# Block attention in four PSUM banks, stepped beside three gate projections; stage boundaries handed over by token half

## The reference

```python
# first block: an MLA mixer and an mLSTM mixer, each followed by
x = _layernorm(ALPHA * x + y, ln_w[layer], ln_b[layer])
...
# second block
mod = c_act @ w_ada[l] + b_ada[l]
sh1, sc1, g1, sh2, sc2, g2 = [m[:, None, :] for m in jnp.split(mod, 6, axis=-1)]
h = rms_norm(x, norm1_w[l]) * (1.0 + sc1) + sh1
proj = h @ w_in[l]
qa, ka, va, qb, kb, vb, ga, gb = jnp.split(proj, offs, axis=-1)
...
ya = global_gqa(qa, ka, va)
yb = neighbourhood_attention(qb, kb, vb, nat_rpb[l])     # reshapes left out
merged = jax.nn.sigmoid(ga) * (ya @ w_oa[l]) + jax.nn.sigmoid(gb) * (yb @ w_ob[l])
x = x + g1 * (merged @ w_out[l])
h2 = rms_norm(x, norm2_w[l]) * (1.0 + sc2) + sh2
ff = (jax.nn.silu(h2 @ w_ffn_gate[l]) * (h2 @ w_ffn_up[l])) @ w_ffn_down[l]
x = x + g2 * ff
```

## Time and profile before

| | |
|---|---|
| median of 3 runs | 2306.06 us (2302.61 to 2310.73) |
| the profiled execution | 2306.09 us |
| its span, first to last instruction | 2304.4 us |
| mean granted clock of PE | 0.981 of full speed |
| busy: PE, PEld, DVE, ACT, POOL | 2233.5, 1884.6, 1495.8, 1007.7, 243.3 us |
| HBM read | 495.34 MB, 216 GB/s |

### The profile page before, as it was taken

How to read it: one execution, slowest core, us unless ns; L and a number is a source line. 1 busy time by engine, 2 the same in 40 slices (tenths; PEclk the granted TensorE clock), 3 DMA queues, 4 the chain that set the end, 5 groups by cost and what they waited for, 6 DMA issues and landing times.

```text
span 2304.4 us, 33253 instructions
## 1 busy us (share of the span) xinstructions
PE 2233.5 (97%) x11044; PEld 1884.6 (82%) x11044; DVE 1495.8 (65%) x1990; ACT 1007.7 (44%) x1248; POOL 243.3 (11%) x425
## 2 busy tenths in 40 slices
PE   8999998999999979999999999999999999999996
PEld 7888776998877769799778888888888888888885
DVE  5666578887776866777676667775665565454544
ACT  5444534454444433434554443444444444343432
POOL 1110011212220030100111111110110010000000
PEclk9999999999999997999999999989999999999998
DMA  8786166887986583767538887755677676665663
GB/s 307 248 242 175 37 228 256 249 265 264 318 278 180 159 243 122 247 184 226 193 106 273 254 261 245 235 207 179 223 256 228 220 258 217 190 206 183 190 197 119
DMA packets 196666, 499.25 MB, mean 217 GB/s; under 512 B 29784, under 2 KB 56536, under 8 KB 195648
## 3 DMA queue, kind: packets, MB, share of 16 engines
q1 hardware_dynamic: 163648, 388.03, 52.3%
q0 software_dynamic: 32896, 109.55, 14.3%
HBM read 495.34 MB, written 2.10 MB: 216 GB/s over the span
## 4 chain that ended last, share of the span: by engine, by line
PE 89%; DVE 4%; DMA 3%; ACT 2%; issue 1%; POOL 0%; DVEq 0%; POOLq 0%; SPq 0%; ACTq 0%
PE ps L1669 72%; PE ps L1678 10%; PE ps L1738 2%; PE ps L1759 1%; DMA ada_raw<-in_w_ada_dram 1%; PE ps L1748 1%; DMA raw<-in_ml_w_in_dram 1%; DVE lo L924 1%; DMA rel<-in_rpbT_dram 1%; PE ps L1829 1%; PE ps L1912 0%; PE ps L1707 0%; DVE acc_g L936 0%; ACT hi L551 0%; PE ps L1968 0%
## 5 line engine op out<-in xcount | busy, mean ns | idle before, releaser
L924 DVE TENSOR_TENSOR lo<-raw,hi 128x1024 fp32r<-128x1024 f32 x732 | 892.8, 1224 | 616.9 <-ACT hi L551 614.6
L551 ACT CAST hi<-raw 128x1024 fp32r<-128x1024 f32 x732 | 765.9, 1051 | 1080.4 <-PE ps L1669 848.2
L1669 PE MATMUL ps<-hi,XH 128*128 128x512 f32 x2080 | 650.6, 393 | 28.8 <-DVE lo L924 22.3
L1669 PE MATMUL ps<-lo,XH 128*128 128x512 f32 x2080 | 646.1, 391 | 0.0
L1669 PE MATMUL ps<-hi,XL 128*128 128x512 f32 x2080 | 645.3, 390 | 0.0
L1669 PEld LDWEIGHTS ps<-hi,XH 128*128 128x128 f32 x2080 | 389.7, 189 | 111.4 <-DVE lo L924 16.2
L1669 PEld LDWEIGHTS ps<-hi,XL 128*128 128x128 f32 x2080 | 392.1, 189 | 82.4
L1669 PEld LDWEIGHTS ps<-lo,XH 128*128 128x128 f32 x2080 | 392.0, 188 | 82.2
L465 POOL DMA_DIRECT2D ada_raw<-in_w_ada_dram x384 | 206.9, 539 | 1575.8 <-DVE acc_s L936 978.2
L936 DVE SCALAR_TENSOR_TENSOR acc_s<-ada_raw,c_act,acc_s 128x512 f32<-128x512 f32 x256 | 191.3, 747 | 14.6 <-DMA ada_raw<-in_w_ada_dram 13.3
L1678 PE MATMUL ps<-XH,hi 128*128 (+1 forms) x512 | 145.0, 283 | 0.7 <-DVE XL L1040 0.7
(11 more groups left out here) (311 smaller groups left out, 1668.3 us busy)
## 6 DMA issues: line engine op xcount, KB each, us to landing
ada_raw<-in_w_ada_dram POOLq DMA_DIRECT2D x384, 256.0 KB, 4.7
raw<-in_w_in_dram SPq DMA_DIRECT2D x136, 512.0 KB, 4.4
raw<-in_ml_w_in_dram SPq DMA_DIRECT2D x128, 512.0 KB, 5.0
raw<-in_w_gate_dram SPq DMA_DIRECT2D x176, 256.0 KB, 3.0
raw<-in_w_up_dram SPq DMA_DIRECT2D x176, 256.0 KB, 3.8
raw<-in_w_down_dram SPq DMA_DIRECT2D x88, 512.0 KB, 4.2
raw<-in_mla_w_in_dram SPq DMA_DIRECT2D x48, 512.0 KB, 5.2
raw<-in_mla_w_out_dram SPq DMA_DIRECT2D x32, 512.0 KB, 4.7
```

What stands on the lines that cost most here:

```text
L551: nc.scalar.copy(hi[:, j, :], raw[:, j, :]).then_inc(hi_ready, 1)
L924: nc.vector.tensor_tensor(lo[:, j, :], raw[:, j, :], hi[:, j, :].bitcast(F32), ALU.subtract) \
L1669: ins = mm(ps[:, o:o + HALF], x, w[:, j, c0:c0 + HALF], start=first, stop=(k == nb * per_block - 1 and x is xl), skip_group_check=True)
```

## The change

Five things are changed. (1) Block attention uses four banks (two for scores, one for transposed probabilities, one for values), and runs as 36 steps, one after each of the first 36 of 48 blocks of ga0, ga1 and gb0, which all use the other four banks. The units with bias come first. DVE normalises the probabilities before they are transposed, and values are computed feature by token, so that the transposes back are gone. The last four blocks of ga0 and ga1 and the first four of the stage after each are worked one token half at a time, in pairs of blocks (`gate_slot`), with the casts of those blocks moved to match (`CASTS`). (2) g1, qaT and kaT stand between blocks of vb, the gates of the second mixer inside mv0. (3) mo1, lo1, wo1 and down1 end with the last four blocks one token half after the other (`half_done`), and residual, statistics and normalising follow by token half. (4) The second eight activation tiles (x1Tb, hTb, h2Tb) are transposed after the fifth block of the stage that needs them, and the first two tiles are split singly. (5) `ADA_BESIDE` is spread anew, POOL's list is reordered, and ACT casts all of lo1 before it waits for `toep` and `rel`.

```diff
-    "x1Ta@1:split4 x1Tb:split4 mlq:taps8 mlk:taps8 mv0:act gates:dve mv1:act mo_0:act mo_1:act mz0:act mz1@0:act "
+    "x1Ta@1:split5 mlq:taps8 x1Tb:split4 mlk@1:taps8 mv0:act gates:dve mv1@1:act mo_0:act mo_1:act mz0:act mz1@0:act "
...
-ADA_BESIDE = {"z0": 16, "z1": 16, "mo0": 16, "mo1": 16, "mlq": 14, "mlk": 14, "mv0": 16, "mv1": 16, "mo_0": 20,
-              "mo_1": 20, "mz0": 6, "mz1": 6, "lo0": 16,
+ADA_BESIDE = {"z0": 16, "z1": 16, "mo0": 16, "mo1": 16, "mlq": 4, "mlk": 12, "mv0": 14, "mv1": 20, "mo_0": 18,
+              "mo_1": 18, "mz0": 6, "mz1": 6, "lo0": 16, "lo1": 14,
...
 # POOL
-            ada_units(5, 7)
+            ada_units(5, 6)
             pool.wait_ge(*complete("gates"))
-            for half in range(2):
-                load("gate_bias", gate_bias[32 * half:32 * half + 8, :], gate_b[8 * half:8 * half + 8, :])
             load("causal", causal[:, :], cst("causal"))
             load("select", select[:, :, :].rearrange(flat), cst("select", 0, 8))
-            ada_units(7, 12)
+            ada_units(6, 11)
             pool.wait_ge(tile_split, SPLIT_BASE["yTb"] + 8)
             load("rows1", *bcast(row_w[:, :], ln_w[1:2, :]))
...
                 load("rel", rel[64 * part + 32:64 * part + 63, :, :], rpbT[:, :, 4:10])
+            ada_units(11, 12)
             pool.wait_ge(*complete("ada1"))
             init_acc(2, acc_s[:, :, :].rearrange(flat), 3 * D, 2 * D, 3)
             ada_units(12, 15)
-            pool.wait_ge(*complete("g1"))
+            ada_units(15, 20)
+            pool.wait_ge(*complete("mTa"))
             init_acc(3, acc_g[:, :], 5 * D, D, 4)
-            ada_units(15, N_UNITS)
+            ada_units(20, N_UNITS)
...
 # ACT, lo1
             first4(B_LO + 16)
+            rest(B_LO + 16, 16)
             act.wait_ge(ev("toep"), 16)
             nc.scalar.copy(toep_r[:, :], toep[:, :]).then_inc(ev("toep_r"), 1)
             act.wait_ge(ev("rel"), 64)
             nc.scalar.copy(rel_parts[:, :, :], rel[:, :, :]).then_inc(ev("rel_hi"), 1)
-            rest(B_LO + 16, 16)
...
 # ACT, the shared slots
+            for slot in range(48):
+                for b in CASTS[slot]:
+                    hi_block(B_MERGE + b, b % RING, landed(B_MERGE + b, b % RING))
+                if slot < 36:
+                    blk_step(slot)
+                if slot in (14, 16):
+                    gate_half("ga0", (slot - 14) // 2, sig_a[0])
+                if slot in (30, 32):
+                    act.wait_ge(A3["summed"], N_A)
+                    gate_half("ga1", (slot - 30) // 2, sig_a[1])
...
 # DVE, mo1
+            quarter("mo1", 0, (0, 1), (ev("mo1_half"), 1))
+            quarter("mo1", 1, (0,), (ev("mo1_three"), 1))
+            quarter("mo1", 1, (1,), complete("mo1"))
+            after(own[0])
+            for tok in range(TOK):
+                mark(nc.vector.bn_aggr(mvar[:, tok, :], st[:, tok, :, :]))
+            after(own[0])
+            rsqrt(2, 1.0, mvar[:, :, 1])
...
 # DVE, lo1 to qa
+            last_residual("lo1", 0)
+            dve.wait_ge(ev("rows1"), 32)
+            x2_rows(0)
+            last_residual("lo1", 1)
+            rms_token(0, 1, ss[:, 0:1])
+            x2_rows(1)
+            rms_token(1, 2, ss[:, 1:2])
+            normalise_second(1)
+            lo_block(B_QA, 0)
             modulation("ada1", "norm1")
-            lo_block(B_QA + 3, 3)
-            split_operand("hTa", "h_full")
-            rest(B_QA, 16, "qa")
+            split_operand(0, "h_full", B_QA)
+            rest_blocks(B_QA, 4, 8, 16, "qa")
+            split_operand(1, "h_full", B_QA)
+            rest_blocks(B_QA, 8, 16, 16, "qa")
...
 # DVE, the shared slots
+            for slot in range(48):
+                name, r = ("ga0", "ga1", "gb0")[slot // 16], slot % 16
+                if slot < 36:
+                    blk_maximum(slot)
+                for b in CASTS[slot]:
+                    lo_block(B_MERGE + b, b % RING)
+                for m in range(ADA_BESIDE[name] * r // 16, ADA_BESIDE[name] * (r + 1) // 16):
+                    ada_block((ADA_FIRST[name] + m) // KD, (ADA_FIRST[name] + m) % KD)
+                blk_divide(slot)
...
 # PE
+            ada_columns("ada1", 8, lambda: (start("hTa"), turn_first("hTa", h_norm, h_ready, first_token)))
+            turn_first("hTa", h_norm, h_ready, second_token)
...
+            def blk_step(i):
+
+                if i == 0:
+                    pe.wait_ge(freed_sem["act"], FREED["vb"][1])
+                if i < 32:
+                    h, t = (i % 16) // 2, slice(i % 2 * P, (i % 2 + 1) * P)
+                    q, k = (qbT[:, h, t], kbT[:, h, :]) if i < 16 else (qaT[:, h, t], kaT[:, h // (N_A // N_KV), :])
+                    if i >= 2:
+                        pe.wait_ge(A3["exped"], i - 1)
+                    o = score_slot(i)
+                    mm(ps[:, o:o + SEQ], q, k, start=True, stop=True, skip_group_check=True).then_inc(A3["scored"], 1)
+                if i >= 4 and i % 2 == 0:
+                    h = (i - 4) // 2
+                    pe.wait_ge(A3["copied"], h + 1)
+                    if h >= 1:
+                        pe.wait_ge(A3["lo"], h)
+                    o = value_slot
+                    for t in range(TOK):
+                        v = vb_tok[:, t, h * HD:(h + 1) * HD] if h < N_A \
+                            else kva_tok[:, t, N_KV + (h - N_A) // (N_A // N_KV), :]
+                        ins = mm(ps[:, o:o + SEQ], v, probT2[:, t, :], start=(t == 0), stop=(t == TOK - 1),
+                                 skip_group_check=True)
+                    ins.then_inc(A3["summed"], 1)
+                if 2 <= i < 34:
+                    u = i - 2
+                    pe.wait_ge(A3["normed"], u + 1)
+                    if u >= 2 and u % 2 == 0:
+                        pe.wait_ge(A3["copied"], u // 2)
+                    for t in range(TOK):
+                        o = turn_slot + t * SEQ + u % 2 * P
+                        ins = nc.tensor.transpose(ps[:, o:o + P], prob2[:, u % 3, t * P:(t + 1) * P], ident[:, :])
+                    ins.then_inc(A3["turned"], 1)
...
+            start("ga0")
+            for slot in range(48):
+                gate_slot(slot)
+                if slot < 36:
+                    blk_step(slot)
```

More of the change, by code:

```diff
@@ L845, in _ @@
+            act.wait_ge(A3["lo"], 2 * N_A)
+            each_tok("gb0", lambda t: sig_b[0][:, t, :], ACT.Sigmoid)
+            rest(B_MERGE + 48, 16)
+            first4(B_MERGE + 64)
+            each_tok("gb1", lambda t: sig_b[1][:, t, :], ACT.Sigmoid)
+            rest(B_MERGE + 64, 8)
             for n in range(3):
@@ L1519, in _ @@
+            rest(B_MERGE + 48, 16, "gb1")
             first4(B_MERGE + 64)
```

601 lines of the change are left out of this document (385 added, 216 removed).

## The result

Predicted: 2294.0 us, range 2280 to 2305. Measured: 2291.23 us, median of 4 runs (2290.34 to 2292.01), against 2306.44 (2302.61 to 2310.73, 4 runs) before. The ratio is 0.9939, with a 95% interval of 0.9924 to 0.9954. The profiled execution of the changed kernel has a span of 2289.3 us and took 2290.99, so it stands for the median.

The account below looks back on a forecast made before the run. PE was taken as nearly always busy, with time only in its waits, half-clock stretches and small work; 6.1-8.9+1.3+9.9+0.5+3.0=11.9 us off 2306.1 gave 2294 us, range 2280 to 2305.

Parts of the forecast that it names:

- mo1 to mlq: From mo1's last matmul to mlq: token 0 finishes early and half the transposes come later, 6.1 us saved.
- small2: Load sent only after ada 79, in mlk: lands about 7 us before it would stop PE, cost 0.
- lo0 to lo1: At lo1's first block: ada 176 queues behind rel loads, stall some 20.5 us instead of 11.35, 8.9 us lost.
- rival (b): Before lo1: ada 176 overtakes the rel loads, 2.6 us lost instead of 8.9, total 2288; chance 0.18.
- Rival (a): At lo1: the ada step stops nothing, 176 in time or index misread, total 2274; chance 0.12.
- lo1 to qa: From lo1's end to qa: fewer transposes first, with 1.3 us for a cast beside POOL's memset; 1.3 us saved.
- Attention: Block attention among gate blocks: PE sets the pace, a pair of slots 7.6 us, 9.9 us saved.
- handovers: Between ga0, ga1 and gb0: ACT's table loads delay the probT copy, 1.5 us twice, 3 us.
- switching: In the attention slots: PE changing between gate block and step shows hidden tails, 2 us taken of up to 12.
- wo1 to ffn0: From wo1's end to ffn0: 17.9 us becomes 17.4 with h2Tb and a cold ffn0, 0.5 us saved.
- End: After the last matmul: token 0's row work goes early and fewer stores leave at once, 3.0 us saved of 17.4.
- rival (d): In the attention slots: DVE becomes the pace, ending slower than before beyond 4.3 us a slot; about 2319, chance 0.05.

Follow-up runs that it names:

- whole_last_blocks: Changed kernel with the last four blocks of mo1, lo1, wo1 and down1 run block by block, both tokens each: 2306.04 us.
- two_ahead: Changed kernel with only ada blocks 176 and 177 issued ahead of the rows and rel loads: 2281.77 us.
- ada_as_before: Changed kernel with the places of the ada steps and the order of POOL's loads as before the change: 2274.66 us.
- small2_earlier: Changed kernel with small2's memset and two loads issued after the first eight ada blocks of unit 4 instead of all sixteen: 2291.01 us.
- before_act_only: Kernel before, with only ACT's casts of lo1's blocks 4 to 15 put ahead of its wait for toep and rel: 2294.93 us.
- rebalanced_rows_after: Changed kernel, POOL's loads as before except rows0 after eight unit 4 ada blocks; ada steps mo0 22, mo1 18, mlq 4, mlk 16; acc_s memset later: 2268.96 us.

## Why the prediction came out, term by term

The sum was 11.9 us and the profiled executions are 15.1 apart.

- **mo1 to mlq**, 6.1 predicted. The end of mo1 to mlq's start fell from 17.4 to 8.9 us. Then mlq to mv0 takes 94.0 to 94.8 us where small2 does not disturb it, against 92.2: 1.75 for x1Tb and a cold start. 8.5 less 1.8 to 2.6 is 5.9 to 6.7: right.
- **small2**, put at 0 with the words that it lands 7 us before it would stop PE. This was wrong. It was issued at 467 and let ACT go at 481.43, 13 us after its second load (468.3). That is at the edge, and the waits at mv0 in kernels with the same code up to there (but for the order at mo1 in whole_last_blocks) were 2.29, 2.05, 1.80, 1.07, 0.89, 0.67 and 0.50 us. The profiled execution lost 2.3 of waiting and some 1.8 of half rate: 4.1.
- **lo0 to lo1**, 8.9 lost. Measured from the end of lo0 to the end of lo1: 56.9 before, 65.1 after, 8.2 lost. The stall was 19.46 against some 20.5. The rows show each step of the argument: the index 176, DVE's order, the queue behind rel. POOL was quicker than I had it (834.97, not 841), and so was PE (lo0 ended at 829.8, not 835.5), and these two errors cancel. two_ahead gave the queue its own test. Of rival (b), the free landing, 5.8 us, nothing was seen: 11.3, 14.4 and 14.7 us. Rival (a), no stall, is what ada_as_before has.
- **lo1 to qa**, 1.3 saved; by the stage 32.9 to 30.6 us, less the 1.4 that qa's start to vb's is longer with hTb in it, 0.9. The memset lies where it was said, but was mis-sized: the cast under it took 2.49 us in the changed kernel and its like 0.29, 2.2 more and not 1.3.
- **Attention**, 9.9 saved. From vb's start to the transposes behind ob1: 360.4 before, 348.7 after, 11.7. PE paces: the pair of slots is 7.67 us, 7.6 predicted. The handovers were mis-sized: PE waits 0.71 and 0.81 us for probT, where 1.5 twice was the term, and both cost 2.0 instead of 3. Of the 2 us for switching, nothing can be seen as such.
- **wo1 to ffn0**, 0.5 saved: 17.8 to 12.7 us, less 1.75 for h2Tb and 2.8 for the cold start of ffn0, 0.6. The sum fits by luck: the stretch came 1.6 us shorter than the 14.3 forecast, and the cold start cost 1.5 more than the 1.3.
- **End**, 3.0 saved: 4.7, 17.4 to 12.7 us. This term was mis-sized. whole_last_blocks gives 4.0 of it back.
- **Before mo1's end**, nothing predicted, 2.6 us gained, and not by the change. The x1 transposes, with the same code and the same wait of 5.3 us in front of them, began at 383.8 in the changed kernel and at 389.5 in small2_earlier, which differs only later on. In the windows from 240 to 262 us, early in latent attention, the granted clock was 0.92 before, 1.00 after, and 0.77 in before_act_only and small2_earlier. PE waits about 1.06 us near 240 us in every one of them, and then the clock stands at the lower level for 3.4 us, for none, and for 10.2 us. At half rate that is 1.7, 0 and 5.1 us: 1.7 of the 2.6, and 5.1 of the 5.7 between 383.8 and 389.5. What decides between the three stays open.

Two slips in the working did no harm: 853.3, 1.5 and 1.2 add up to 856.0, which is 9.1 lost and not 8.9, and rival (d) ends slower than before from 4.1 us a slot on (3.8 and 11.9/36), not 4.3.

With the small2 cost of 4.1 against the chance gain of 2.6, and the attention and the end 3.5 better than forecast, the time lands 3 us below 2294. So the mechanism was right, and part of the closeness is luck. The balance that the prediction drew is right: of some 23 us that the change gains, 8.2 go back at one load that was put behind others. What it did not ask is how much is to be had by mending that: rebalanced_rows_after is 22 us below the changed kernel, by nothing but the order of POOL's work and the places of the ada steps.

Left open: the rest of the 5.3 us that 10 more steps in mlq cost (99.3 against 94.0; waits for lo and the clock make 3.5); and whether POOL's loads are what slows the weight blocks early in lo1, where a wait of 2.0 to 2.5 us stays in every mended version.

## What to carry to other kernels

When work is moved between stages, count the index of the last item that each stage consumes against the last that its loader has issued by then: two items too few made a stall of 19.5 us, and a load needed earlier than before, with two large ones in front of it, one of 6.6 us. On one queue put what is needed first in front, not what is small: rows and tables and, last, four loads of 5.8 KB in fine pieces held the 256 KB load behind them back by 5 to 9 us. And where row work follows a matmul stage, let the last blocks finish one token half early: at four places this was worth 14.8 us here, more than the attention's 11.7.
